# Starting three of four attentions ahead of their last heads, with a reordered opening and other copies in the delta rule's ends

## What is computed

```python
# first attention: rotary embedding on the latent tokens only
q = rms_norm(q, q_gain); k = rms_norm(k, k_gain)
o = attend(apply_rope(q_l), concat(apply_rope(k_l), k_c), v); o_ctx = attend(q_c, k_c, v_c)
# delta rule, per token and head
S = S * w - (S @ kk) (kk * a)^T + v k^T ; y = S @ r
# third attention: q = w_uq rank, last 32 of 96 features rotated (latent only)
# fourth: softmax over [q.k * scale + bias, q.k_ctx * scale], then its values
```

## Time and profile before

| | |
|---|---|
| median of 3 runs | 2582.37 us (2579.70 to 2583.63) |
| the profiled execution | 2580.51 us, of which its span 2577.6 us |
| mean granted TensorE clock | 0.987 of full speed |
| busy in the span | TensorE matmuls 95%, weight loads 77%, VectorE 65%, ScalarE 41%, GpSimd 15% |
| the chain that ended last | TensorE 81%, VectorE 9%, ScalarE 3% |
| moved from HBM | 320 MB, 125 GB/s over the span |

### The profile page before, as it was taken

One profiled execution on the slowest core, in us unless ns is written; L12 is line 12 of the kernel. 1 busy time (PEld: TensorE's weight loads), 2 busy tenths in 40 slices (PEclk: granted clock), 3 DMA queues, 4 the chain that ended last, 5 costly groups with the idle time before them and its releaser, 6 DMA issues.

```text
span 2577.6 us, 46166 instructions
## 1 busy us (share of the span) xinstructions
PE 2438.6 (95%) x17946; PEld 1984.0 (77%) x17946; DVE 1679.6 (65%) x2771; ACT 1055.6 (41%) x1744; POOL 375.7 (15%) x340
## 2 busy tenths in 40 slices
PE   6999999988898999999999999889999999899987
PEld 3888888857676788888788888679997875577866
DVE  2877787665555787788877754665555335665665
ACT  4222224365344622222522224455455244545354
POOL 2000001023253200000100001010013600121052
PEclk8999999999999999999999999999999999999999
DMA  6655663200000365566455542224562321013301
GB/s 248 243 190 194 194 205 116 89 22 3 4 4 21 120 208 192 194 196 203 164 195 190 192 136 94 93 72 158 180 179 99 98 86 50 1 66 125 127 19 50
DMA packets 88421, 323.34 MB, mean 125 GB/s; under 512 B 9712, under 2 KB 10864, under 8 KB 87504
## 3 DMA queue, kind: packets, MB, share of 16 engines
q1 hardware_dynamic: 86864, 310.68, 37.3%
q0 software_dynamic: 1408, 10.59, 1.1%
HBM read 320.18 MB, written 1.05 MB: 125 GB/s over the span
## 4 chain that ended last, share of the span: by engine, by line
PE 81%; DVE 9%; ACT 3%; issue 3%; DMA 1%; DVEq 1%; POOL 0%; POOLq 0%; ACTq 0%; SPq 0%
PE bank L502 22%; PE bank L503 22%; PE bank L504 22%; PE bank L1380 1%; DVE row_statistics L1434 1%; DVE weights_hi_lo L408 1%; DMA weight_ring<-stream_k 1%; PE bank L1389 1%; PE bank L2213 1%; ACT weights_hi_lo L403 1%; PE bank L1405 1%; PE bank L2219 1%; PE bank L1809 1%; PE bank L2849 1%; DVE work L3199 1%
## 5 line engine op out<-in xcount | busy, mean ns | idle before, releaser
L403 ACT ACTIVATE weights_hi_lo<-weight_ring 128x1024 fp32r<-128x1024 f32 (+1 forms) x381 | 396.6, 1042 | 1086.4 <-PE bank L504 1061.0
L408 DVE TENSOR_TENSOR weights_hi_lo<-weight_ring,weights_hi_lo 128x1024 fp32r<-128x1024 f32 (+1 forms) x374 | 455.2, 1217 | 480.7 <-ACT weights_hi_lo L403 479.1
L502 PE MATMUL bank<-input_hi,weights_hi_lo 128*128 128x512 f32 (+1 forms) x2032 | 743.5, 366 | 19.0 <-DVE input_lo L813 12.6
L503 PE MATMUL bank<-input_lo,weights_hi_lo 128*128 128x512 f32 (+1 forms) x2032 | 740.2, 364 | 0.0
L504 PE MATMUL bank<-input_hi,weights_hi_lo 128*128 128x512 f32 (+1 forms) x2032 | 740.0, 364 | 0.0
L502 PEld LDWEIGHTS bank<-input_hi,weights_hi_lo 128*128 128x128 f32 x2032 | 386.4, 190 | 85.9 <-issue 22.9
L503 PEld LDWEIGHTS bank<-input_lo,weights_hi_lo 128*128 128x128 f32 x2032 | 386.4, 190 | 59.8 <-issue 0.7
L504 PEld LDWEIGHTS bank<-input_hi,weights_hi_lo 128*128 128x128 f32 x2032 | 386.3, 190 | 59.9
L502 PE MATMUL bank<-hidden_hi_lo,weights_hi_lo 128*128 128x512 f32 (+1 forms) x952 | 342.8, 360 | 6.0 <-DVE weights_hi_lo L408 3.0
L503 PE MATMUL bank<-hidden_hi_lo,weights_hi_lo 128*128 128x512 f32 (+1 forms) x952 | 339.7, 357 | 0.0
L504 PE MATMUL bank<-hidden_hi_lo,weights_hi_lo 128*128 128x512 f32 (+1 forms) x952 | 339.7, 357 | 0.0
(11 more groups left out here) (524 smaller groups left out, 2946.6 us busy)
## 6 DMA issues: line engine op xcount, KB each, us to landing
weight_ring<-stream_k SPq DMA_DIRECT2D x498, 512.0 KB, 3.5
weight_ring<-stream_f SPq DMA_DIRECT2D x64, 448.0 KB, 3.4
weight_ring<-stream_f SPq DMA_DIRECT2D x32, 512.0 KB, 4.0
extra_tiles<-condrows POOLq DMA_DIRECT2D x3, 1024.0 KB, 8.9
constants<-consts POOLq DMA_DIRECT2D x1, 2112.5 KB, 9.2
residual_stream<-xin SPq DMA_DIRECT2D x1, 2048.0 KB, 11.6
work<-nabias POOLq DMA_DIRECT2D x1, 2048.0 KB, 9.5
residual_stream<-ctx POOLq DMA_DIRECT2D x1, 1024.0 KB, 5.9
```

What stands on the lines that cost most here:

```text
L403: act.activation(split_place(place)[:, 0, 0:words], w[:, 0:words], ACT.Copy).then_inc(hi_ready, 1)
L408: eng.tensor_tensor(split_place(place)[:, 1, 0:words], ring[:, n % RING, 0:words], split_place(place)[:, 0, 0:words].bitcast(F32), ALU.sub ...
L502: pe.matmul(out, weights[:, 0, w], x_hi, start=first, stop=False)
L503: pe.matmul(out, weights[:, 0, w], x_lo, start=False, stop=False)
```

## The change

- In the opening ScalarE makes the high part of slab 0 alone ahead of the tiles, that of slab 1 behind tile 0 and that of slab 2 behind tile 4. VectorE makes their low parts behind tiles 1 and 5 of its own loop.
- Even attention: sum, root, norm and cosine of tile 4 move into the ahead functions, its bank becomes 3 instead of 1. The turns go in the order 4, 0, 1, 2, 3. Step 0 of the attention comes after three turns on TensorE, after the first sine on VectorE and before the copy of the values on ScalarE. Pair 1 waits for the values and for the first maximum, pair 2 for `heads_ready`.
- mla attention: pair `it` waits for heads up to 2 it + 1 alone; VectorE takes the first maximum between heads 6 and 7.
- na attention: pairs 0 and 1 are scored ahead of both transposes; these now use banks 4 to 7 one after the other. ScalarE copies the values, takes the exponentials of pair 0, and then copies `GVTOK` in VectorE's place; pair 2 waits for that.
- Delta rule's ends: VectorE takes the outputs first and raises a new semaphore, `outputs_added`, for which ScalarE's copy of the state inputs waits; `group_added` follows `RR` and `EIT`. TensorE waits for `group_added` behind the next group's first products instead of ahead of them.

```diff
@@ norm_scalar, norm_vector
+        SPLITS_BEHIND = (0, 4)
             if n == 0:
                 first_mods_scalar(act, (3,))
-                for k in range(3):
-                    first_split_scalar(act, stage, k)
+                first_split_scalar(act, stage, 0)
...
+                if n == 0 and kt in SPLITS_BEHIND:
+                    first_split_scalar(act, stage, 1 + SPLITS_BEHIND.index(kt))
...
             if n == 0:
-                first_splits_vector(dve, stage, (1,))
                 first_mods_vector(dve)
...
-                if n == 0 and kt == 1:
-                    first_splits_vector(dve, stage, (2,))
+                if n == 0 and kt - 1 in SPLITS_BEHIND:
+                    first_splits_vector(dve, stage, (1 + SPLITS_BEHIND.index(kt - 1),))
@@ attend_tensor
             for it in range(n + 3):
+                if which == "even" and it == 0:
+                    pe.wait_ge(qk_normed, 5)
+                if which == "even" and it == 1:
+                    pe.wait_ge(max_ready, 1)
+                    pe.wait_ge(values_ready, 1)
+                if which == "even" and it == 2:
+                    pe.wait_ge(heads_ready, 1)
+                if which == "mla" and it < 4:
+                    pe.wait_ge(q_rotated, ODD_HEADS + 2 * it + 2)
+                if which == "na" and it == 2:
+                    pe.wait_ge(gv_ready, 1)
@@ even heads
-        EVEN_BANKS = (4, 5, 6, 7, 1)
+        EVEN_BANKS = (4, 5, 6, 7, 3)
+        EVEN_TURNS = (4, 0, 1, 2, 3)
...
-        def even_heads_scalar(act):
-            even_root(act, 4)
+        def even_heads_scalar(act, attention):
+            next(attention)
...
-            even_sum(pe, 4)
-            for i in range(4):
+            for i in EVEN_TURNS[:3]:
                 even_turn(pe, i)
             pe.wait_ge(*linear_copied(0, 20))
+            next(attention)
+            for i in EVEN_TURNS[3:]:
+                even_turn(pe, i)
...
-        def even_heads_vector(dve):
-            for i in range(4):
+        def even_heads_vector(dve, attention):
+            even_sine(dve, 4)
+            next(attention)
+            for i in EVEN_TURNS[1:]:
                 even_sine(dve, i)
             dve.drain()
-            for i in range(4):
+            for i in EVEN_TURNS:
                 even_rotated(dve, i)
-            even_norm(dve, 4)
...
@@ mla_heads_vector, for h in range(8)
+                if h == 6:
+                    next(attention)
@@ na heads
-            turn_values(pe, BIG[:, 16:20, :], 4, 0).then_inc(values_turned, 1)
+            next(attention)
+            next(attention)
             pe.wait_ge(spans_used, 2)
+            turn_values(pe, BIG[:, 16:20, :], 4, 4).then_inc(values_turned, 1)
+            pe.wait_ge(values_ready, 4)
             turn_values(pe, BIG[:, 4:8, :], 4, 4).then_inc(gv_turned, 1)
...
             ins.then_inc(values_ready, 1)
+            next(attention)
+            act.wait_ge(gv_turned, 1)
+            for tt in range(TT):
+                ins = act.activation(GVTOK[:, tt, :], pb[4 + tt][:, :], ACT.Copy)
+            ins.then_inc(gv_ready, 1)
@@ wkv_start_tensor
             if g:
-                pe.wait_ge(group_added, 2 * g - 1)
                 pe.wait_ge(inputs_copied, 2 * g - 1)
...
             within(n0)
+            if g:
+                pe.wait_ge(group_added, 2 * g - 1)
@@ wkv_scalar
-                    act.wait_ge(group_added, 2 * g + u + 1)
+                    act.wait_ge(outputs_added, 2 * g + u + 1)
@@ wkv_group_vector
-                dve.tensor_tensor(by_half(RR[:, j, :]), by_half(RR[:, j, :]), bank_pair(x, 0), ALU.add)
-                dve.tensor_tensor(by_half(EIT[:, j, :]), bank_pair(x, 1), on_cells(TAB("ident64")), ALU.add)
...
-                ins.then_inc(group_added, 1)
+                ins.then_inc(outputs_added, 1)
+                dve.tensor_tensor(by_half(RR[:, j, :]), by_half(RR[:, j, :]), bank_pair(x, 0), ALU.add)
+                dve.tensor_tensor(by_half(EIT[:, j, :]), bank_pair(x, 1), on_cells(TAB("ident64")), ALU.add)\
+                   .then_inc(group_added, 1)
```

More of the change, by code:

```diff
@@ L1366, in attend_tensor @@
             n = len(pairs)
-            pe.wait_ge(heads_ready, a + 1)
-            pe.wait_ge(values_ready, a + 1)
+            if which == "odd":
+                pe.wait_ge(heads_ready, a + 1)
+                pe.wait_ge(values_ready, a + 1)
             if which == "mla":
+                pe.wait_ge(heads_ready, a + 1)
+                pe.wait_ge(values_ready, a + 1)
                 pe.wait_ge(rope_spread, 8)
-                pe.wait_ge(q_rotated, ODD_HEADS + 8)
+            if which == "na":
+                pe.wait_ge(heads_ready, a + 1)
             for it in range(n + 3):
+                if which == "even" and it == 0:
[9 more added lines that the diff above has]
+                    pe.wait_ge(gv_ready, 1)
                 if it < n:
@@ L1578, in even_heads_tensor @@
             mm.then_inc(values_turned, 1)
-            even_turn(pe, 4)
         def even_norm(dve, i):
@@ L1817, in mla_heads_tensor, with mla_heads_vector @@
                     pe.matmul(pb[h][:, TC:T], C("rotm"), WORK[:, h, TC:T], start=True, stop=True).then_inc(q_turned, 1)
-        def mla_heads_vector(dve):
+        def mla_heads_vector(dve, attention):
             all_copied(dve, 2, 1)
@@ L1857, in na_heads_vector @@
             dve.drain().then_inc(heads_ready, 1)
[L1858 to L1861, removed]
         def add_neighbours(pool, x, y, before, after):
@@ L1926, in build @@
         solved, solved_copied = sem("right_sides_solved"), sem("solutions_copied")
-        group_ready, group_added = sem("unit_outputs"), sem("unit_outputs_added")
+        group_ready, group_added = sem("unit_outputs"), sem("unit_state_factors_added")
+        outputs_added = sem("unit_outputs_added")
         inputs_copied = sem("state_inputs_copied")
@@ L1999, in wkv_ahead_scalar @@
             even_square(act, 4)
-            for i in range(4):
+            for i in range(5):
                 even_root(act, i)
@@ L3231, in _ @@
             linear_tensor(pe, 0, lambda r: wkv_ahead_tensor(pe, r))
-            even_heads_tensor(pe)
-            for _ in attend_tensor(pe, 0):
+            attention = attend_tensor(pe, 0)
+            even_heads_tensor(pe, attention)
+            for _ in attention:
                 pass
@@ L3258, in _ @@
             linear_tensor(pe, 3, lambda r: gla_gates_tensor(pe) if r == 1 else None)
-            na_heads_tensor(pe)
-            for _ in attend_tensor(pe, 3):
+            attention = attend_tensor(pe, 3)
+            na_heads_tensor(pe, attention)
+            for _ in attention:
                 pass
@@ L3275, in _ @@
             linear_vector(dve, 0, wkv_ahead_vector(dve))
-            even_heads_vector(dve)
-            for it, _ in enumerate(attend_vector(dve, 0)):
+            attention = attend_vector(dve, 0)
+            even_heads_vector(dve, attention)
+            for it, _ in enumerate(attention, 1):
                 if it in (2, 5):
@@ L3296, in _ @@
             linear_vector(dve, 2, mla_ahead_vector(dve))
-            mla_heads_vector(dve)
-            for _ in attend_vector(dve, 2):
+            attention = attend_vector(dve, 2)
+            mla_heads_vector(dve, attention)
+            for _ in attention:
                 pass
@@ L3321, in _ @@
             linear_scalar(act, 0, wkv_ahead_scalar(act))
-            even_heads_scalar(act)
-            for it, _ in enumerate(attend_scalar(act, 0)):
+            attention = attend_scalar(act, 0)
+            even_heads_scalar(act, attention)
+            for it, _ in enumerate(attention, 1):
                 if it in (4, 7):
@@ L3349, in _ @@
             linear_scalar(act, 3, gla_ahead_scalar(act))
-            na_heads_scalar(act)
-            for it, _ in enumerate(attend_scalar(act, 3)):
+            attention = attend_scalar(act, 3)
+            na_heads_scalar(act, attention)
+            for it, _ in enumerate(attention, 1):
                 if it in (4, 7):
```

18 lines of the change are left out of this document (8 added, 10 removed).

## The result

The changed kernel ran at a median of 2564.65 us (2561.99 to 2566.26, four runs) beside 2581.03 us of the kernel before (2576.93 to 2583.63, four runs): ratio 0.9937, 95% interval 0.9925 to 0.9949. A second set gave 2567.41 us and 0.995 (0.9937 to 0.9963). Over all nine runs its median is 2566.3, the kernel before stays at 2580.1 to 2580.2 in every larger set. The gain is some 14 us, where 9.3 was forecast and 12.5 was the sum of all upper bounds.

A forecast was written before the change was run, and what follows sets the result against it. TensorE, busy 95% of the span, was taken to bound the kernel. Terms 2.5 + 2.8 + 2.7 - 0.4 + 1.7 = 9.3 us took the median of 2582.37 to 2573.1 us, range 2569.5 to 2578.5.

The forecast's parts named there:

- The opening: Opening's reordered splits: TensorE starts its first product 2.5 us earlier, bounds 1.0 to 3.3.
- Even: Even attention's start: pair 2 waits only for `heads_ready` and begins 2.8 us earlier, bounds 1.8 to 3.8.
- the moved sum: Even attention: the sum of tile 4, now ahead of the last product, moves no later point.
- mla: mla attention's start: pairs 0 and 1 fit before the last heads, pair 2 starts 2.7 us earlier, bounds 1.5 to 2.9.
- The step that failed: Behind the edited places no engine waits for a clock time or fixed transfer, so each gain reaches the end in full.
- The delta rule: Delta rule's ends: waits of VectorE and TensorE for the state inputs' copy go, 1.7 us gained, bounds 1.0 to 2.0.
- na: na attention: pair 2 waits for ScalarE's copies, 0.4 us lost, bounds 0.5 gained to 2.5 lost.
- A: Even and mla attentions: half the early start comes back, they give 2.8 us together, 2575.8 us; chance 0.18.
- B: Even and mla attentions: no early start, na loses 2.5 us, 2579 us, no change; chance 0.16.
- C: Opening: late tiles starve TensorE, its clock stays at 1.2 GHz, each matmul costs 0.2 us more, 2585 us; chance 0.04.

The follow-up runs named there:

- the single part's run: The kernel before with the early start of the even attention alone, including its moved sum, root, norm and turns: 2580.87 us (11 runs), ratio 1.0001.
- `no_mla`: The changed kernel with the mla attention's early start undone: 2572.81 us (12 runs).

## Why na costs more, and what even still leaves

The na part left out: 

> The changed kernel with the na attention's early start undone. By the stage from 2440 to 2500 us over ten traces (60.9 us without the part, 62.0 with it) it is 1.1 us faster than the changed kernel, 2565 against 2566; by my term 0.4 faster. If instead the part only shifts the clock's fall, its stage takes 60.4 to 61.2 us and the whole time is the changed kernel's within 2 us.

Measured: 2567.22 us (5 runs), ratio 0.9952 (0.9938 to 0.9966), its stage 61.3 with a longer fall of the clock. In the whole it can't be told from the changed kernel. The wait put behind pair 2's scores:

```
-                if which == "na" and it == 2:
-                    pe.wait_ge(gv_ready, 1)
...
+                if which == "na" and u == 0:
+                    pe.wait_ge(gv_ready, 1)
                 if 0 <= u < n:
                     pe.wait_ge(probs_scaled, u0 + u + 1)
```

> The changed kernel; in the na attention TensorE waits for the copies of the gated values behind the scores of pair 2 instead of ahead of them (the copies free the banks of the transposes, not those of the scores). If the part's loss (1.1 us in the stage from 2440 to 2500 us) is the wait that was put ahead of pair 2, its scores start 2.1 us earlier and the stage is 1 to 2 us shorter than in the changed kernel at the same place of the clock's fall. If ScalarE's copies, which pair 1's exponentials queue behind, are the loss, the stage gains less than 0.3.

Measured: 2565.44 us (6 runs), the stage 59.9 us. And even's pair 2 let go ahead of the other queries' additions:

```
-                if which == "even" and it == 2:
-                    pe.wait_ge(heads_ready, 1)
+                if which == "even" and it in (2, 4):
+                    pe.wait_ge(heads_ready, it // 2)
...
-            for i in EVEN_TURNS:
+            for i in EVEN_TURNS[:2]:
                 even_rotated(dve, i)
             dve.drain().then_inc(heads_ready, 1)
+            for i in EVEN_TURNS[2:]:
+                ins = even_rotated(dve, i)
+            ins.then_inc(heads_ready, 1)
```

> The changed kernel; in the even attention pair 2 waits for the rotation of the keys and the first queries alone, and the other three queries' additions (1.2 us) run on VectorE behind. If VectorE's additions are what ends TensorE's wait for pair 2 (2.1 us in the changed kernel's trace), pair 2 starts 1.2 us earlier and the stage from 534 to 600 us takes about 62.2 instead of 63.4. If the attention is bound by VectorE's operations behind, the 1.2 us come back and the stage stays at 63.4. In the whole time, 1.2 us is too little to see.

Measured: 2566.51 us (6 runs), the stage 62.7 against a mean of 63.3: pair 2 waited 1.05 instead of 2.10, and half of it reached the stage's end. Both edits together:

> The changed kernel with both edits (na's later wait, even's split rotation): the version that should beat both kernels if both edits hold, 2563 to 2565 us against 2566 of the changed one. If neither holds, the same as the changed one.

Measured: 2563.59 us (2559.52 to 2568.63, 6 runs), ratio to the kernel before 0.9941 (0.9927 to 0.9956). Stages: even 62.7, na 58.8. With no fall of the clock in either trace, na took 60.7 in the changed kernel and 58.8 here, so the wait ahead of pair 2 was worth 1.9. TensorE's waits there, in the changed kernel and in this one:

```profile
PE bank L1396 <- ACT spare_tiles L1876: 2.2, 1, 2.2
```

```profile
PE bank L1405 <- ACT spare_tiles L1879: 1.1, 1, 1.1
```

With even's 0.6 the stages make it 2.5 us shorter than the changed kernel at equal clock; the medians say 2.7 (2566.3 over nine runs), with ranges that overlap. It is the best supported version, not one shown to be faster in the whole.

The even part left out: 

> The changed kernel with the even attention's early start undone. Its stage (534 to 600 us) should be 66.2 instead of 63.4 us. If the stage's gain passes to the end, the kernel is 2.9 us slower than the changed one, 2569; if the clock's falls behind it (690, 798, 1631 us) take it back, as the single part's run suggests (0.7 slower than before, for a stage 2.9 shorter), it is at 2566.

Measured: 2569.12 us (6 runs), 2.9 over the changed kernel, and the stage took 66.4. By these medians, whose ranges overlap, the even part's gain reached the end. With the single part's nothing, it stays open how much of a gain ahead of many falls of the clock arrives on average.

## Why the prediction was wrong

- **The opening** (2.5): right, 2.5 in the wait and 2.6 in the stage's mean, with GpSimd slowing VectorE's low part (2.28 instead of 0.88) as priced by the row beside it. The Trainium skill's rule in GPSIMD Engine Reference, section Specifications, that such operations contend, holds for the tile as for the split.
- **Even** (2.8): right in size, 2.75 from 300 to 600 us, and partly by luck. Pair 2 came 0.6 us later than forecast (7.2 to 7.5 us after the turns in the five traces with the part, 6.7 by the sum), since the additions took 3.0 us. But the trace that the forecast was read from was a short one: pair 2 began 9.6 us after the turns there and in the second trace, and 10.1 in the five other traces without the part, where the clock fell ahead of the first scores. The statement that the moved sum moves no later point is off by the 0.2 us above.
- **mla** (2.7, upper bound 2.9): right for what was priced. Pair 2 began where it was put, 2.8 us earlier. Mis-sized was the rest of the term: I let the clock's fall in as a risk of the lower bound alone, and not as a cost of the kernel before that an earlier start would lift. The stage gave 3.8, and its size follows the fall at the attention's head: without the part 74.5 us in the two traces with a short fall and 75.7 in the five with a long one, with it 71.3 in the four without a fall and 73.0 in the one with a short one.
- **The step that failed** is the sentence that no engine waits for a clock time behind these places, so that each gain passes to the end as it is. TensorE's clock is such a thing: 2.9 us came from 2214 to 2300 us, where nothing was edited, by being reached at another moment. That even's gain was lost in the same way where it stood alone is likely from its trace, and not shown.
- **The delta rule** (1.7, at least 1.0): 0.9. The waits went as said, but I counted the second scan's, which is covered by TensorE's late product.
- **na** (0.4 lost): 0.8 lost in the mean. The mechanism is the one named: the added wait ahead of pair 2. The steps of that sum end at 2465.7 and not at 2466.1 (2463.6 plus 2.06), so the 0.4 was not worked out from them. What the mean adds is the clock: the stage with the part took 60.7 us without a fall and 63.0 or 63.1 with a long one. With a short fall it took 61.1 with the part (`no_mla`) against 60.4 to 61.0 without, so at an equal clock little is lost. The wait did not have to stand there.
- **The rivals**: A (half comes back), B (no early start) and C (TensorE starved, slower) all looked for something that takes the gain back. None let the clock add to it. C's premise, that its slow matmuls cost the full 0.2 us each, falls too: the opening at the low clock costs at most about 1 us, and TensorE waits for no tile there. The Trainium skill, TensorE: Matmul & The Clock Gate, section HAM oscillation, has waits longer than the work keep the clock down; no stretch here ran so from end to end.

Of the 14 us, 12.0 are placed in stages. Some 0.8 lie outside the span: the kernel before spends 2.6 us there in the mean of 27 runs, the changed one 1.8 in each of its nine, for a reason that no run shows. The last 1 us is within what the falls of the clock move between runs (the kernel before alone: 2573.7 to 2583.2) and stays open.

## What to carry to other kernels

Idle time of TensorE has a second price, the clock behind it; ask at each gap whether the row behind it shows 1.2 GHz, and put into the upper bound what those matmuls would take at 2.4 GHz, if nothing else feeds them late. A shift of some microseconds can lift or bring a fall far behind the edit, so compare the same instruction's start, stage by stage, in several traces before a part is called good or bad. When a wait is split off a gate, place it at the first instruction whose buffer needs it, and not at the loop's step.

## What the runs showed of the hardware

The same stretch, with the same wait of 1.0 us ahead, ran at 2.4 or at 1.2 GHz depending on when it was reached; stages without an edit then take one of two times (17.5 or 15.95 us from 2214 to 2232) and hardly anything between. What TensorE did ahead, 1.58 us busy of 3.00 with no wait above 1.02, was the same in both cases. Two traces of one kernel differ in the same way. That this makes most of the kernel before's spread (2573.7 to 2583.2 us over 27 runs) is likely, and only argued; for it speaks that the five runs with the highest mean granted clock (0.988) took 2575.2 us in the mean and the other 22 took 2580.7.
